# Copying out and laying down a forget gate's running sum before a memory step's second mix instead of after the step

## The chip, the cores and the metric

The kernel runs on one NeuronCore of a Trainium2 chip. The metric is the device time of one execution in microseconds, lower is better. TensorE does all matrix products and transposes and writes only to PSUM (eight banks of 128 partitions by 512 float32). ScalarE (ACT), VectorE (DVE), GpSimd (POOL) and SyncE (SP, which here only issues loads and stores) each run their own list of instructions in order, and meet through semaphores: an instruction that waits holds up all that stands behind it on its engine.

## The reference, cut to what matters

The model has two layers over 512 tokens of width 1024. The second one is what the change is in:

```
kvf = x @ kv_w                                   # keys, values and 12 forget-gate logits
f_logit = kvf[..., 2 * D_MIX:] + kv_b_f
logcum  = cumsum(log_sigmoid(f_logit), axis=1)   # running sum over the 512 tokens
z = x @ b_w_q                                    # queries: 12 heads, and 4 memory heads
mix = fox_attention(q, k_sh, v_sh, logcum)       # logit[t,s] = q_t.k_s/8 + logcum[t] - logcum[s]
mo  = memory_attention(qm, mk, mv)               # 4 heads, 256 memory tokens
y = concat([mix, mo]) @ w_o; LN; squared-ReLU MLP; LN
```

logcum[t] is constant along a row of the softmax and drops out, so only logcum[s] has to reach the scores: it does as an extra row of the key operand.

## The kernel before, in words

Float32 precision is made from float32r halves: each operand is split into hi (a copy that rounds, by ScalarE) and lo (whole minus hi, by VectorE, `rest` at L1462), and each product is three matmuls (hi·hi, hi·lo, lo·hi), all at L513.

Every engine has its own hand-written list. The second layer's mixer is a chain of **steps**, `pair_step`, one per pair of heads; a step handles eight units u (head u // 4, block u % 4 of 128 queries): scores into `sc[u % 2]`, maximum, exponential, normalization, transpose, split; then `attend(s, 0)` and `attend(s, 1)`, the probabilities times the values into the banks `pv`, which are copied out as `mix_hi` (ScalarE `attended`, L1137) and `mix_lo` (VectorE `attended`, L1545). Between the units TensorE runs **fillers**: parts of the next projections (weights `w_hi`, `w_lo`, into the banks `proj`).

The step before the six forget-gate pairs is `STEP_B`, the **double memory step**: it does all four memory heads at once (`double(s)` is true), a unit being one block of 128 queries for two heads. Its fillers make the query, key and value projections of the first forget-gate pair. At its end TensorE does, in this order: `attend` 0, `turn` 6, filler 8, `turn` 7, `cumulate()`, filler 9, `attend` 1 (the second mix), `turn_values`, and then the first filler and the scores of the next step.

`cumulate()` (L973) makes the running sum: eight matmuls of the split log gates with a triangular matrix into `sc[0]`, which signal `cum_done`. The way from there to the next step's scores:

1. ScalarE copies `sc[0]` to `cum` (L1434) and signals `f_act` 4.
2. VectorE waits for that and forms the lo part in rows 32 to 63 and 96 to 127 (`rest`, twice), signal `f_step` 6.
3. VectorE `cum_rows(pair)` (L1609 to L1616) waits for `f_step` 6 and writes the pair's rows into the key operand `kc` (two multiplications by `head_rows`), signal `row_ready`.
4. TensorE `scores` (L586) at unit 0 of the next step waits for `row_ready` (L598). At unit 1 it waits for `vt_ready` (L604): the value tile, turned by `turn_values` into `sc[1]` for this step, split into `v_hi` (L1194) and `v_lo` (L1657).

In the kernel before, 1 to 3 stand behind `pair_step(Pos(STEP_B), ...)` on ScalarE (L1433, L1434) and VectorE (L1951 to L1955), so behind the second mix's `mix_hi`, `mix_lo`, `v_hi` and `v_lo`. In the later steps `cum_rows(values)` is called inside `pair_step`, before `attended(s, 1)` (L1652). ScalarE's list goes on with the next step's weight split (`prepare`, L1066), VectorE's with the maximum (L1521) of unit 0. SyncE's loads wait for `w_split`, which VectorE's weight splits signal.

Of the kernel before, what the change touches and what calls it, by code (L numbers as in the profile page):

```python
# [63 lines left out]
def trunk_kernel(nc, x, mem, a_w_in, a_sgu_ln_g, a_sgu_ln_b, a_w_s, a_b_s, kv_w, kv_b_f, b_w_q,  # L64
# [41 lines left out]
    STEP_A, STEP_B, STEP_FOX, STEP_LAST = 0, 2, 3, 8  # L106
# [12 lines left out]
    with ctx:  # L119
        def psum(name):  # L120
            return ctx.enter_context(nc.psum_tensor(name, [P, 512], F32))

        def sem(name):
            return ctx.enter_context(nc.semaphore(name))
# [4 lines left out]
        def put(name, shape, dtype, offset=None):  # L129
            size = 4  # L130
            for n in shape[1:]:
                size *= n
            if offset is None:
                offset = base[0]
                base[0] += (size + 63) // 64 * 64
            assert offset + size <= nc.sbuf_usable_end, (name, offset + size)
            return nc.alloc_sbuf_tensor_at(name, shape, dtype, offset=offset)
# [82 lines left out]
        cum = put("cum", [P, T], F32R, B0 + 20 * K1)  # L220
# [53 lines left out]
        sc = [psum("sc0"), psum("sc1")]  # L274
# [33 lines left out]
        f_done, f_out, lf_zeroed, f_step, f_act, cum_done = sem("f_done"), sem("f_out"), sem("lf_zeroed"), sem("f_step"), sem("f_act"), sem("cum_done")  # L308
# [63 lines left out]
        def tr_index(s, u):  # L372
            return s.times(8, T_STEP[s.base >= STEP_B] + u)
# [4 lines left out]
        def fox(s):  # L378
            return STEP_FOX <= s.base <= STEP_LAST

        def double(s):

            return s.trip is None and s.base == STEP_B
# [13 lines left out]
        def keys(s, u):  # L397

            return u % TT + 1 if fox(s) else 2 * MT if double(s) else MT
# [659 lines left out]
        def _(act):  # L1059
            def prepare(b):  # L1060

                if b.trip is None and b.base >= B_DN[1][1] + 2 * KT:
                    return
                act.wait_ge(w_landed[b.slot], b.half(2) * 16)
                wait(act, w_used, space(b))
                act.copy(weights(b)[0], w_raw[:, b.slot]).then_inc(w_hi_ready, 1)  # L1066
# [11 lines left out]
            def turned_hi(t, target, source=None):  # L1078

                act.wait_ge(tr_done, t.at(1))  # L1080
                act.copy(target, tr[t.slot][:, :] if source is None else source).then_inc(tr_hi, 1)
# [50 lines left out]
            def turned_probs(s, u):  # L1132
                n, t = keys(s, u), tr_index(s, u)
                turned_hi(t, turned_places(s, u)[0],
                          tr[t.slot][:, 0:n * P].rearrange("p (j t) -> p j t", j=n))
# [26 lines left out]
            def pair_step(s, b=None, g=None, values=None, late=None):  # L1162

                mixing = b is not None and s.base < STEP_B
                reading = b is not None and s.base >= STEP_B
                for u in range(8):
                    if mixing and u in (0, 3, 6):
                        prepare(b.plus(u // 3 + 1))
                    if reading and u in (0, 4, 7):
                        prepare(b.plus((u + 2) // 3 + (u == 0)))  # L1170
                    if late is not None and u == 1:
                        prepare(late)
                    if ahead(s):
                        exponentials(s, u)
                    if u >= 2:
                        turned_probs(s, u - 2)
                    if not ahead(s):
                        exponentials(s, u)
                    if mixing and u in (2, 5):
                        step_projection(s, b.plus(u // 3), g.plus(u // 3), u // 3)  # L1180
                    if reading and u == 2:
                        for head in range(2):
                            fox_head(b, g, 0, head)
                    if reading and u in (5, 6):
                        fox_head(b.plus(1), g.plus(1), 1, u - 5)
                attended(s, 0)
                turned_probs(s, 6)
                turned_probs(s, 7)
                if b is not None:
                    step_projection(s, b.plus(2), g.plus(2), 2)  # L1190
                attended(s, 1)
                if values is not None:
                    act.wait_ge(vt_done, values.at(1))
                    act.copy(v_hi[:, values.slot], values_bank(s)[:, :].rearrange("p (t c) -> p t c", t=TT)).then_inc(vt_hi, 1)  # L1194
# [234 lines left out]
            for r in range(0, P, 32):  # L1429
                last = act.copy(lf_hi[:, :, r:r + HEADS], f_sp[:, :, :])  # L1430
            last.then_inc(f_act, 1)
            pair_step(Pos(STEP_B), Pos(B_FOX), Pos(G_FOX), values=Pos(0))
            act.wait_ge(cum_done, 1)  # L1433
            act.copy(cum[:, :], sc[0][:, :]).then_inc(f_act, 1)  # L1434
            with act.Fori(0, 2) as i:
                for j in range(2):
                    pair_step(Pos(STEP_FOX + j, i, 2), Pos(B_FOX + 3 * (j + 1), i, 6),
# [21 lines left out]
        def _(dve):  # L1459
            def rest(target, whole, hi):  # L1460

                return dve.tensor_tensor(target, whole, hi.bitcast(F32), ALU.subtract)  # L1462
# [146 lines left out]
            def cum_rows(pair):  # L1609

                dve.wait_ge(f_step, 6)
                for head in range(2):
                    rows = other_rows(head)
                    last = dve.tensor_scalar(kc[rows, pair.slot, head, :], cum[rows, :].bitcast(F32),
                                             head_rows[rows, bass.ds(pair.at(), 1)], None, ALU.mult)
                last.then_inc(row_ready, 1)  # L1616

            def pair_step(s, b=None, g=None, values=None, late=None):
                mixing = b is not None and s.base < STEP_B
                reading = b is not None and s.base >= STEP_B  # L1620
                if ahead(s):
                    row_max(s, 0)
                for u in range(8):
                    if not ahead(s):
                        row_max(s, u)
                    if mixing and u in (0, 3, 6):
                        prepare(b.plus(u // 3 + 1))
                    if reading and u in (0, 4):
                        prepare(b.plus(u // 4 + 1))
                    if late is not None and u == 1:  # L1630
                        prepare(late)
                    if ahead(s):
                        if u + 1 < 8:
                            row_max(s, u + 1)
                        normalize(s, u)
                    if u >= 2:
                        turned_probs(s, u - 2)
                    if not ahead(s):
                        normalize(s, u)
                    if s.base == STEP_A and 1 <= u <= TT:  # L1640
                        gate_norm(u - 1)
                    if reading and u in (2, 3):
                        fox_query(values, g, u - 2)
                    if reading and u == 6:
                        fox_key(values, g.plus(1), 0)
                turned_probs(s, 6)
                attended(s, 0)
                turned_probs(s, 7)
                if reading:
                    prepare(b.plus(3))  # L1650
                    fox_key(values, g.plus(1), 1)
                if fox(s) and values is not None:  # L1652
                    cum_rows(values)
                attended(s, 1)
                if values is not None:
                    dve.wait_ge(vt_hi, values.at(1))
                    rest(v_lo[:, values.slot], values_bank(s)[:, :].rearrange("p (t c) -> p t c", t=TT),  # L1657
                         v_hi[:, values.slot]).then_inc(vt_ready, 1)
# [235 lines left out]
            for j in range(PAIRS + 1):  # L1894
                if j == 2:
                    prepare(Pos(B_WO[0] + 1))
                for c in range(2):
# [6 lines left out]
                    for head in range(2):  # L1904
                        rows = slice(head * HALF, (head + 1) * HALF)
                        last = dve.tensor_tensor(gated(j, c)[rows].rearrange("p (n t) -> p n t", n=2), mixed[rows, :, head],
                                                 u_t[rows, j, c * 2 * P:(c + 1) * 2 * P].rearrange("p (n t) -> p n t", n=2), ALU.mult)
# [39 lines left out]
            for r in range(0, P, 32):  # L1947
                last = rest(lf_lo[:, :, r:r + HEADS], f_sp[:, :, :], lf_hi[:, :, r:r + HEADS])
            last.then_inc(f_step, 1)
            pair_step(Pos(STEP_B), Pos(B_FOX), Pos(G_FOX), values=Pos(0))  # L1950
            dve.wait_ge(f_act, 4)  # L1951
            for r in (32, 96):
                last = rest(cum[r:r + 32, :], sc[0][r:r + 32, :], cum[r:r + 32, :])
            last.then_inc(f_step, 1)
            cum_rows(Pos(0))  # L1955
            with dve.Fori(0, 2) as i:
                for j in range(2):
                    pair_step(Pos(STEP_FOX + j, i, 2), Pos(B_FOX + 3 * (j + 1), i, 6), Pos(G_FOX + 3 * (j + 1), i, 6),
                              values=Pos(j + 1, i, 2))
# [171 lines left out]
```

## Time and profile before

| | |
|---|---|
| device time, median of 3 runs | 1207.45 us (1206.73 to 1207.56) |
| the profiled execution | 1207.21 us |
| its span, first to last instruction | 1205.5 us |
| TensorE busy | 1161.2 us, 96% |
| VectorE busy | 632.7 us, 52% |
| ScalarE busy | 491.2 us, 41% |
| GpSimd busy | 129.3 us, 11% |
| mean granted TensorE clock | 0.992 of full speed |
| the chain that ended last | TensorE 74%, VectorE 4%, ScalarE 4%, issue 3% |

The span runs from the first to the last recorded instruction; the rest of the device time lies around it. Busy shares are means over stages with different limits. The double memory step lies at about 602 to 637 us of the span, the six forget-gate pairs follow until about 790 us, then the output projection and the second MLP. "PE" is TensorE's matmuls, "PEld" its weight loads.

### The profile page before, as it was taken

How to read it: one execution, taken by the hardware profiler on the slowest of the kernel's cores; microseconds unless marked ns; L12 is line 12 of the kernel's file. 1: busy time of each engine (PE TensorE's matmuls, PEld its weight loads, DVE VectorE, ACT ScalarE, POOL GpSimd, SP SyncE). 2: the span in 40 equal slices, each digit the busy share in tenths (PEclk: the TensorE clock that was granted, in tenths of full speed). 3: DMA queues.
4: the chain of work that ended last, by engine and by line, in shares of the span. 5: the costliest groups of instructions: out<-in, count | busy, mean ns of one | idle time of the engine just before them, and what ended most of it. 6: DMA issues, size and time to landing. Idle time of an engine off the chain costs nothing.

```text
span 1205.5 us, 16763 instructions
## 1 busy us (share of the span) xinstructions
PE 1161.2 (96%) x5888; PEld 976.6 (81%) x5888; DVE 632.7 (52%) x1032; ACT 491.2 (41%) x852; POOL 129.3 (11%) x156
## 2 busy tenths in 40 slices
PE   5998999999999999999998999999999999999997
PEld 5777779888888888789877888878888888888886
DVE  4477766644332445345576777866544323445226
ACT  4445535634211333224665555635543212334120
POOL 2300025100000000023300000026200000000000
PEclk9999999999999999999998999999999999999999
DMA  7422122333323333332311122212333333333332
GB/s 219 134 70 71 53 90 86 88 89 103 105 87 104 88 101 91 105 88 73 86 35 53 54 70 62 60 53 84 93 104 90 102 104 87 88 98 93 105 105 87
DMA packets 185590, 107.22 MB, mean 89 GB/s; under 512 B 4482, under 2 KB 180162, under 8 KB 185540
## 3 DMA queue, kind: packets, MB, share of 16 engines
q1 hardware_dynamic: 180112, 99.36, 28.5%
q10 hardware_dynamic: 5428, 7.18, 1.9%
q8 instruction: 32, 0.52, 0.2%
q14 instruction: 18, 0.15, 0.0%
HBM read 104.43 MB, written 2.10 MB: 88 GB/s over the span
## 4 chain that ended last, share of the span: by engine, by line
PE 74%; DVE 4%; ACT 4%; issue 3%; POOL 1%; DMA 0%; DVEq 0%; ACTq 0%; POOLq 0%; SPq 0%
PE proj L513 59%; PE pv L513 3%; PE sc L513 2%; PE proj L846 2%; PE pv L846 2%; PE tr L846 2%; PE sc L846 2%; PE tr L561 1%; DVE w_lo L1462 1%; ACT w_hi L1066 1%; ACT x L1232 1%; ACT x_hi L1234 1%; POOL total L2054 0%; DVE split_lo L1462 0%; POOL total L2064 0%
## 5 line engine op out<-in xcount | busy, mean ns | idle before, releaser
L1462 DVE TENSOR_TENSOR w_lo<-w_raw,w_hi 128x1024 fp32r<-128x1024 f32 x173 | 219.6, 1270 | 172.3 <-ACT w_hi L1066 124.2
L513 PE MATMUL proj<-x_hi,w_hi 128*128 128x512 f32 (+1 forms) x768 | 300.5, 393 | 1.9 <-ACT relu L1097 1.0
L513 PE MATMUL proj<-x_hi,w_lo 128*128 128x512 f32 (+1 forms) x768 | 295.9, 386 | 0.0
L513 PE MATMUL proj<-x_lo,w_hi 128*128 128x512 f32 (+1 forms) x768 | 289.8, 384 | 0.0
L1066 ACT CAST w_hi<-w_raw 128x1024 fp32r<-128x1024 f32 x160 | 166.9, 1044 | 168.6 <-PE proj L513 166.9
L513 PEld LDWEIGHTS proj<-x_hi,w_hi 128*128 128x128 f32 x768 | 146.1, 190 | 28.9 <-ACT x_hi L1234 2.2
L513 PEld LDWEIGHTS proj<-x_hi,w_lo 128*128 128x128 f32 x768 | 145.8, 190 | 29.2
L513 PEld LDWEIGHTS proj<-x_lo,w_hi 128*128 128x128 f32 x768 | 143.1, 189 | 25.7
L513 PE MATMUL proj<-h_hi,w_hi 128*128 128x512 f32 (+1 forms) x384 | 146.4, 381 | 2.5 <-DVE w_lo L1462 2.5
L513 PE MATMUL proj<-h_lo,w_hi 128*128 128x512 f32 (+1 forms) x384 | 146.0, 380 | 0.0
L513 PE MATMUL proj<-h_hi,w_lo 128*128 128x512 f32 (+1 forms) x384 | 146.0, 380 | 0.0
L1755 DVE TENSOR_TENSOR h_raw<-relu 128x512 f32<-128x512 f32 x64 | 44.3, 692 | 157.7 <-ACT relu L1097 157.7
L1097 ACT ACTIVATE relu<-proj 128x512 f32<-128x512 f32 x64 | 38.2, 597 | 196.0 <-PE proj L513 196.0
L513 PEld LDWEIGHTS proj<-h_hi,w_hi 128*128 128x128 f32 x384 | 72.2, 188 | 16.8 <-DVE w_lo L1462 3.1
L513 PEld LDWEIGHTS proj<-h_lo,w_hi 128*128 128x128 f32 x384 | 72.2, 188 | 13.8
L513 PEld LDWEIGHTS proj<-h_hi,w_lo 128*128 128x128 f32 x384 | 72.2, 188 | 13.7
L1129 ACT ACTIVATE probs<-sc,neg_max 128x128 f32<-128x128 f32 (+2 forms) x64 | 33.0, 516 | 55.9 <-DVE neg_max L1521 54.9
L2005 POOL TENSOR_TENSOR x_lo<-x,x_hi 128x256 fp32r<-128x256 f32 (+1 forms) x56 | 48.5, 875 | 58.0 <-ACT x L1230 24.8
L1462 DVE TENSOR_TENSOR h_lo<-h_raw,h_hi 128x512 f32 (+1 forms) x64 | 44.3, 692 | 14.9 <-ACT h_hi L1246 14.4
L2054 POOL TENSOR_TENSOR total<-x 128x512 f32<-128x512 f32 x3 | 4.5, 1499 | 440.9 <-DVE x L1672 440.9
L513 PE MATMUL proj<-mix_hi,w_hi 128*128 128x256 f32 (+1 forms) x128 | 45.8, 358 | 2.5 <-DVE w_lo L1462 2.2
L1665 DVE SCALAR_TENSOR_TENSOR x<-x,proj 128x512 f32 (+1 forms) x22 | 15.1, 687 | 61.0 <-PE proj L513 61.0
(344 smaller groups left out, 1805.4 us busy)
## 6 DMA issues: line engine op xcount, KB each, us to landing
w_raw<-in_w_up SPq DMA_DIRECT2D x64, 512.0 KB, 4.0
w_raw<-in_w_down SPq DMA_DIRECT2D x64, 512.0 KB, 3.6
w_raw<-in_w_o SPq DMA_DIRECT2D x16, 512.0 KB, 3.6
w_raw<-in_a_w_in SPq DMA_DIRECT2D x14, 512.0 KB, 3.8
w_raw<-in_kv_w SPq DMA_DIRECT2D x12, 512.0 KB, 3.9
w_raw<-in_mem_w_kv SPq DMA_DIRECT2D x8, 512.0 KB, 4.9
w_raw<-in_b_w_q SPq DMA_DIRECT2D x8, 512.0 KB, 3.6
x_nat<-in_x ACTq DMA_DIRECT2D x2, 1024.0 KB, 11.4
```

Source lines behind the costliest of these rows:

```text
L513: last = pe.matmul(target, lhs, rhs, start=start and n == 0, stop=stop and n == len(terms) - 1)
L561: last = pe.transpose(tr[t.slot][0:n, at:at + rows], piece, ident[0:rows, 0:rows])
L846: last = pe.matmul(rows_of[t][n][:, :], lhs, rhs, start=False, stop=stop and m == 2, skip_group_check=True)
L1066: act.copy(weights(b)[0], w_raw[:, b.slot]).then_inc(w_hi_ready, 1)
L1097: act.activation(target, proj[g.slot][:, 0:target.shape[-1]], function).then_inc(proj_free[g.slot], 1)
L1129: act.activation(probs[:, u % 2, 0:n], sc[u % 2][:, 0:n], ACT.Exp, bias=neg_max[:, u:u + 1], accum_out=row_sum[:, u:u + 1]).then_inc(exp_d ...
L1232: act.activation(x32[:, k, own], x32[:, k, own], ACT.Identity, **gain).then_inc(fin_ready, 1)
L1234: act.copy(x_hi[:, k, own], x32[:, k, own]).then_inc(x_hi_ready, 1)
L1462: return dve.tensor_tensor(target, whole, hi.bitcast(F32), ALU.subtract)
L1665: dve.scalar_tensor_tensor(out=tile if target is None else target, in0=tile, scalar=ALPHA if first else 1.0, in1=proj[g.slot][:, :], op0=A ...
L1755: dve.tensor_tensor(raw, wide, wide, ALU.mult).then_inc(relu_sq, 1)
L2005: pool.tensor_tensor(x_lo[:, k, own], x32[:, k, own], x_hi[:, k, own].bitcast(F32), ALU.subtract).then_inc(x_ready, 1)
```

## The change

ScalarE's copy moves from behind the step to a place in it ahead of the value projection's copy (`step_projection`) and of the second mix's. VectorE's two subtractions and `cum_rows` move to ahead of the second mix's `mix_lo`, behind the key's second half (`fox_key`). The condition of the `cum_rows` call widens so that it holds for the double step too. No instruction, wait or buffer is added or dropped, and TensorE's, GpSimd's and SyncE's lists are as before.

```diff
 # ScalarE, pair_step
                 attended(s, 0)
                 turned_probs(s, 6)
                 turned_probs(s, 7)
+                if double(s):
+                    act.wait_ge(cum_done, 1)
+                    act.copy(cum[:, :], sc[0][:, :]).then_inc(f_act, 1)
                 if b is not None:
                     step_projection(s, b.plus(2), g.plus(2), 2)
                 attended(s, 1)
 # ScalarE, the list
             pair_step(Pos(STEP_B), Pos(B_FOX), Pos(G_FOX), values=Pos(0))
-            act.wait_ge(cum_done, 1)
-            act.copy(cum[:, :], sc[0][:, :]).then_inc(f_act, 1)
 # VectorE, pair_step
                 if reading:
                     prepare(b.plus(3))
                     fox_key(values, g.plus(1), 1)
-                if fox(s) and values is not None:
+                if double(s):
+                    dve.wait_ge(f_act, 4)
+                    for r in (32, 96):
+                        last = rest(cum[r:r + 32, :], sc[0][r:r + 32, :], cum[r:r + 32, :])
+                    last.then_inc(f_step, 1)
+                if s.base >= STEP_B and values is not None:
                     cum_rows(values)
                 attended(s, 1)
 # VectorE, the list
             pair_step(Pos(STEP_B), Pos(B_FOX), Pos(G_FOX), values=Pos(0))
-            dve.wait_ge(f_act, 4)
-            for r in (32, 96):
-                last = rest(cum[r:r + 32, :], sc[0][r:r + 32, :], cum[r:r + 32, :])
-            last.then_inc(f_step, 1)
-            cum_rows(Pos(0))
```

## Rows read from the trace of the kernel before

**Rows 1.** Waits of TensorE, whole span: who waited, for whom, total us, times, longest.
```profile
PE sc L513 <- DVE kc L1614: 3.5, 1, 3.5
```
**Rows 2.** TensorE's timeline, end of the double step: start us, duration us, instruction, [idle before <-releaser].
```profile
629.24 0.22 PE L513 MATMUL sc<-tri_r,lf_hi 128*128 128x128 f32 x1
629.30 0.27 PE L513 MATMUL sc<-tri_r,lf_lo 128*128 128x128 f32 x1
...
636.32 0.39 PE L513 MATMUL proj<-x_lo,w_hi 128*128 128x512 f32 x1
636.54 0.40 PE L513 MATMUL proj<-x_hi,w_lo 128*128 128x512 f32 x1
640.45 0.44 PE L513 MATMUL sc<-kc,qc 128*128 128x128 f32 x1 [3.51 <-DVE kc L1614]
```
**Rows 3.** VectorE's timeline there, same columns.
```profile
632.35 0.70 DVE L1462 TENSOR_TENSOR kc<-proj,ks 64x512 fp32r<-64x512 f32 x1
635.66 1.39 DVE L1462 TENSOR_TENSOR mix_lo<-pv,mix_hi 64x512 fp32r<-64x512 f32 x2 [2.61 <-ACT mix_hi L1142]
637.08 0.69 DVE L1462 TENSOR_TENSOR v_lo<-sc,v_hi 128x512 fp32r<-128x512 f32 x1
637.80 1.40 DVE L1462 TENSOR_TENSOR cum<-sc,cum 32x512 fp32r<-32x512 f32 x2
639.23 0.98 DVE L1614 TENSOR_SCALAR kc<-cum,head_rows 64x512 fp32r<-64x512 f32 x2
```
**Rows 4.** ScalarE's timeline there.
```profile
627.86 1.11 ACT L1081 CAST pn_hi<-tr 128x512 fp32r<-128x512 f32 x2
631.73 0.60 ACT L1097 ACTIVATE v_tmp<-proj 128x512 f32<-128x512 f32 x1 [2.76 <-PE proj L513]
634.45 1.17 ACT L1142 CAST mix_hi<-pv 64x512 fp32r<-64x512 f32 x2 [2.13 <-PE pv L513]
...
636.13 0.59 ACT L1434 CAST cum<-sc 128x512 fp32r<-128x512 f32 x1
636.61 1.06 ACT L1066 CAST w_hi<-w_raw 128x1024 fp32r<-128x1024 f32 x1
```
**Rows 5.** GpSimd's timeline, its last instruction before the next step.
```profile
624.31 0.61 POOL L2102 CAST ks<-ks 64x512 fp32r<-64x512 f32 x1 [1.93 <-ACT ks L1159]
```
**Rows 6.** TensorE's timeline, one step later (the second forget-gate pair), and the third's start.
```profile
669.38 0.39 PE L513 MATMUL proj<-x_hi,w_lo 128*128 128x512 f32 x1
669.60 0.22 PE L513 MATMUL sc<-kc,qc 128*128 128x128 f32 x1
...
671.99 0.28 PE L513 MATMUL sc<-kc,qc 128*128 128x256 f32 x1
...
673.73 0.27 PE L561 MATMUL tr<-ident,probs 128*128 128x128 f32 x1
...
696.10 0.22 PE L513 MATMUL sc<-kc,qc 128*128 128x128 f32 x1
```
**Rows 7.** VectorE's timeline in that step, from unit 0's maximum.
```profile
670.08 0.29 DVE L1521 TENSOR_REDUCE neg_max<-sc 128x1 f32<-128x128 f32 x1 [0.54 <-PE sc L513]
670.29 1.22 DVE L1462 TENSOR_TENSOR w_lo<-w_raw,w_hi 128x1024 fp32r<-128x1024 f32 x1
...
671.62 0.29 DVE L1537 TENSOR_SCALAR probs<-probs,inv_sum 128x128 f32<-128x128 f32 x1
```
**Rows 8.** Windows: us, then busy (instructions) of PE, PEld, DVE, ACT, POOL, clock granted, DMA share, GB/s.
```profile
636.00:639.20 3.20, 0.94 (x5) 0.42 (x3) 3.11 (x5) 1.67 (x3) 0.00 (x0) 1.00 0.00 0
639.20:646.00 6.80, 5.55 (x16) 4.71 (x17) 2.80 (x7) 0.46 (x2) 0.00 (x0) 0.50 0.27 77
547.00:550.50 3.50, 1.83 (x16) 1.63 (x15) 3.25 (x3) 1.17 (x2) 1.05 (x1) 1.00 0.01 4
799.60:803.00 3.40, 3.40 (x10) 2.62 (x9) 0.34 (x1) 0.00 (x0) 0.00 (x0) 0.51 0.87 245
844.00:847.40 3.40, 3.40 (x18) 3.40 (x17) 1.46 (x5) 1.28 (x2) 0.34 (x1) 0.50 0.90 266
```
**Rows 9.** TensorE's timeline: three other pauses.
```profile
549.18 0.39 PE L513 MATMUL proj<-h_hi,w_hi 128*128 128x256 f32 x1 [1.67 <-DVE w_lo L1462]
798.26 0.50 PE L513 MATMUL proj<-mix_hi,w_hi 128*128 128x512 f32 x1 [1.76 <-DVE w_lo L1462]
843.58 0.38 PE L513 MATMUL proj<-x_hi,w_hi 128*128 128x256 f32 x1 [0.44 <-ACT x_hi L1234]
```

## The prediction

> **What bounds the kernel now.** I read the table of engine shares first. TensorE is busy 1161.2 of 1205.5 us, so the kernel is a stream of matmuls with 44.3 us of holes, and a change that leaves TensorE's list alone can gain only by closing holes, or by what a hole does to the clock. The list of TensorE's waits came second: one of the holes is a single wait of 3.5 us for `kc`, written by the line of `cum_rows` [rows 1]. Third, the timelines of the engines around it. TensorE issues the last filler matmul at 636.54 and the next step's first score matmul at 640.45, idle 3.51 us between [rows 2]. In that time VectorE works without a break: `mix_lo`, `v_lo`, `cum`, `kc`, from 635.66 to 640.2 [rows 3]. But what it does from 637.80 on, the running sum, has had its input in PSUM since 629.30 + 0.27 = 629.57 [rows 2]: it is late because of its place in the list and not because of data. Fourth, the windows by clock: at 636.00 to 639.20 TensorE is busy 0.94 of 3.20 us at full clock (2.4 GHz), and then, from 639.20 to 646.00, the granted clock is 0.50 (1.2 GHz) [rows 8]. So the hole costs twice: its own length, and a slow stretch behind it.
>
> **The moved work on ScalarE.** One copy, 0.59 us alone, 0.48 from its start to the next one's [rows 4]. Before, it stands at 636.13, behind `v_hi`. In its new place ScalarE is free at 627.86 + 1.11 = 628.97, the data is there at 629.57, so it runs from about 629.6 to 630.2. Behind the new wait on ScalarE stand the value projection's copy `v_tmp`, then `mix_hi` and `v_hi`. `v_tmp` waits for TensorE until 631.73 after 2.76 us of idleness [rows 4], so the copy lies wholly in that idleness with 1.5 us left. That cover cannot go away by itself, since TensorE runs `cumulate()` before the filler that `v_tmp` waits for. If it did, each 0.1 us would delay `v_tmp` by 0.1, for which TensorE waits in `turn_values`. Cost taken: 0, with 0 and 0.5 us (the whole copy exposed) as ends. At the old place the copy's absence lets `w_hi` start 0.48 earlier, at 636.13, which nobody awaits that early: a gain of 0.
>
> **The moved work on VectorE.** Two subtractions and two multiplications, from 637.80 to 639.23 + 0.98 = 640.21, 2.41 us in all [rows 3]. In the new place they follow the key's second half, which ends at 632.35 + 0.70 = 633.05. The wait for the copy (630.2) is long met. So they run from 633.05 to about 635.47. Behind them stands `mix_lo`, which waits for ScalarE's `mix_hi` until 635.66 after 2.61 us of idleness [rows 3]. The 2.41 us fit into the 2.61 with some 0.2 us left. That is a narrow fit, so what if it fails: `mix_lo` and `v_lo` end later by the excess. `v_lo` ends at 637.08 + 0.69 = 637.77. It is wanted by the scores of unit 1, which in the undisturbed step come 671.99 - 669.60 = 2.39 us behind those of unit 0 [rows 6], so at 636.77 + 2.39 = 639.16 in the new kernel. There are 1.4 us of slack behind the 0.2. Cost taken: 0. Ends: 0, and 1.0 us if the moved work took 2.6 us longer than its rows. No queue of DMA is passed: the change issues none. SyncE's loads wait for weight splits, and the last one of the step stands ahead of the moved work on VectorE.
>
> **What goes.** With `row_ready` at 635.5, TensorE doesn't wait at unit 0. The other things awaited there are earlier: GpSimd's last copy of key rows ended at 624.92 [rows 5], and the key bank came free with the subtraction that ended at 633.05 [rows 3]. The score matmul then follows the filler at the filler's own pace: 636.54 - 636.32 = 0.22 in the step itself, 669.60 - 669.38 = 0.22 one step later [rows 2, 6]. I take 636.54 + 0.23 = 636.77. First term: 640.45 - 636.77 = **3.68 us**.
>
> Second term, the slow stretch. From the first score matmul of this step to that of the next one it takes 669.60 - 640.45 = 29.15 us; the following step, same instructions and granted the full clock, takes 696.10 - 669.60 = 26.50 [rows 2, 6]. If the hole goes and the clock stays up, the first step takes 26.50 too: **2.65 us**. This agrees with the windows: 5.55 us of busy time at half clock is 2.8 us of excess [rows 8].
>
> What is late next? VectorE, relative to TensorE. In the undisturbed step it starts unit 0's maximum 0.48 us after the first score matmul, splits a weight tile, and finishes the normalized probabilities at 671.62 + 0.29, so 2.31 us after it. TensorE wants them for its transpose at 673.73, 4.13 us after it [rows 6, 7]. Here `v_lo` holds VectorE until 637.77, 1.0 us after the score matmul, so all of this slides by 0.5 us, or 0.7 with a step of the loop's own instructions, against a slack of 1.8. The weight tile itself has its `w_hi` at 636.13 + 1.06 = 637.2, before VectorE comes to it. I therefore expect no new hole of more than 0.2 us. Of all later waits none is on an absolute time: loads wait for splits, splits for weights used, so the whole rest moves up with TensorE.
>
> **The sum.** 3.68 + 2.65 = 6.33 us. The profiled execution took 1207.21 us (a span of 1205.5 and 1.7 around it), which gives 1200.88; the median of the runs lies 0.24 higher, so the forecast is 1207.45 - 6.33 = **1201.1 us**.
>
> **The clock, page against row.** The trace shows full clock during the 3.51 us pause and half clock behind it until 646.00. It also shows half clock behind a pause of 1.76 us (799.60 to 803.00) and behind one of 0.44 (844.00 to 847.40), but full clock around one of 1.67 at 549 [rows 8, 9]. So the length of a pause alone does not say whether the clock falls. The Trainium skill, "TensorE: Matmul & The Clock Gate", section "What's actually happening", says that the gate's looks are free-running, not tied to the kernel's own start. By that rule a program that reaches its later pauses 6.3 us earlier may lose the clock at other ones than now. The trace, with its three unlike cases, agrees as far as it goes.
>
> **Rivals.**
>
> *A, only the hole goes.* The double step has short pauses of its own and many transposes, and the clock could fall somewhere near even without the hole, as it did behind the 0.44 us pause [rows 9]. Against it: from 628 to 636.8 TensorE has no pause at all in its timeline, and with the hole closed it goes on at the same density. Then only 3.68 is gained: 1203.8 us.
>
> *B, the later slow stretches change.* Each of the two at 799.60 and 844.00 lasts 3.4 us at half clock [rows 8], so one more or one less is worth 1.7 us. One less: 1207.45 - 6.33 - 1.7 = 1199.4; one more: 1202.8. The stretch at 844 follows a pause of 0.44 us and looks marginal, the pause of 1.67 at 549 lies before the change and stays as it is. I hold one less for somewhat more likely than one more.
>
> *C, no effect.* The wait moves to another operand of the same scores, or `cum_rows` is held by something that I don't see. Against it: every other input is there by 633.05. The time stays within 0.2% of 1207.45, the most that a measurement of this kernel can't tell from no change (2.4 us).
>
> *D, slower.* The place is VectorE's list ahead of the second mix. If the moved work, reading PSUM while ScalarE and TensorE use their banks, ran so long that `v_lo` came late for unit 1's scores, the hole would reappear there. To eat the gain it must reopen a hole of 3.68 us with its slow stretch: `v_lo` not before 639.16 + 3.68 = 642.8, 5.1 us later than now, so the moved work would need 2.41 + 0.2 + 5.1 = 7.7 us instead of 2.41. At 9 us the time would be 1208.7. For it speaks only that the fit is narrow; against it that ScalarE's and TensorE's lists show nothing that touches `sc[0]` at 633 to 635.5.
>
> **How the numbers follow.** Forecast, both terms and later clock as now: 0.62. B: 0.20 (0.12 for one less, 0.08 for one more). A: 0.11. C: 0.05. D: 0.02. All of the forecast, B and A is more than 0.2% faster, which gives 0.93 faster, 0.05 the same, 0.02 slower. The range holds the forecast, B on both sides and A: from 1199.2 (B with one stretch less, less 0.2 for the spread of the runs) to 1203.9 (A).
>
> **What would show it.** In the new profile `cum` on ScalarE starts at about 629.6 and on VectorE at about 633.1, and `kc` of L1614's successor ends by 635.5 with `mix_lo` still at 635.7: if `mix_lo` has moved, the VectorE fit was wrong. TensorE's wait for `kc` is gone from the list, the first score matmul stands at 636.8, and the windows from 636 to 646 have clock 1.00. If the step from there to the next takes 29 us, the second term was wrong and A holds. If a wait for `v_lo` or for the probabilities appears at 638 to 641, the sum is too large by its length. A difference of 1.7 us that appears only behind 790 us is B.

## The result, and the profile after

The changed kernel takes 1200.39 us (median of 6 runs, 1199.33 to 1200.48) against 1207.22 us for the kernel before on the same chip (6 runs, 1206.17 to 1208.16). The ratio is 0.9946, 95% interval [0.9933, 0.9958]: 6.5 us less, between 5.1 and 8.1. The forecast was 1201.1 and faster. Measured again on another chip, the changed kernel took 1200.95 us (median of 5 runs, 1199.09 to 1204.40) against 1205.69 (13 runs), ratio 0.9963 [0.9948, 0.9977]: 4.5 us less, between 2.8 and 6.3; a sixth run took 4067.55 us, for a reason that nothing here shows, and is left out as a slow one. The two intervals overlap from 5.1 to 6.3 us. The traces of the kernel before, further down, show how much of its time changes from one execution to the next.

TensorE's timeline of the changed kernel, where [rows 2] had the pause (called the hole from here on):

```profile
637.06 0.39 PE L513 MATMUL proj<-x_lo,w_hi 128*128 128x512 f32 x1
637.29 0.40 PE L513 MATMUL proj<-x_hi,w_lo 128*128 128x512 f32 x1
637.52 0.22 PE L513 MATMUL sc<-kc,qc 128*128 128x128 f32 x1
...
639.91 0.28 PE L513 MATMUL sc<-kc,qc 128*128 128x256 f32 x1
```

The first score matmul comes 0.23 us behind the filler's last one. This execution reached the double step 0.77 us later than the other (where it lost that is shown in the last section), so it stands at 637.52 and not at 636.77. The next pair's follows at 663.98.

VectorE's timeline there, against [rows 3]:

```profile
633.10 0.70 DVE L1463 TENSOR_TENSOR kc<-proj,ks 64x512 fp32r<-64x512 f32 x1
633.83 1.39 DVE L1463 TENSOR_TENSOR cum<-sc,cum 32x512 fp32r<-32x512 f32 x2
635.25 0.98 DVE L1615 TENSOR_SCALAR kc<-cum,head_rows 64x512 fp32r<-64x512 f32 x2
636.40 1.39 DVE L1463 TENSOR_TENSOR mix_lo<-pv,mix_hi 64x512 fp32r<-64x512 f32 x2 [0.17 <-ACT mix_hi L1142]
637.83 0.69 DVE L1463 TENSOR_TENSOR v_lo<-sc,v_hi 128x512 fp32r<-128x512 f32 x1
638.44 0.28 DVE L1522 TENSOR_REDUCE neg_max<-sc 128x1 f32<-128x128 f32 x1
```

The four moved operations fill what was 2.61 us of idleness ahead of `mix_lo`, and 0.17 us of it are left. `mix_lo` has not moved: 636.40 less 0.77 is 635.63, against 635.66.

ScalarE's timeline, against [rows 4]:

```profile
630.35 0.59 ACT L1191 CAST cum<-sc 128x512 fp32r<-128x512 f32 x1 [0.64 <-PE sc L513]
632.47 0.60 ACT L1097 ACTIVATE v_tmp<-proj 128x512 f32<-128x512 f32 x1 [1.54 <-PE proj L513]
635.20 1.18 ACT L1142 CAST mix_hi<-pv 64x512 fp32r<-64x512 f32 x2 [2.13 <-PE pv L513]
636.40 0.59 ACT L1197 CAST v_hi<-sc 128x512 fp32r<-128x512 f32 x1
636.88 1.06 ACT L1066 CAST w_hi<-w_raw 128x1024 fp32r<-128x1024 f32 x1
```

The copy waits 0.64 us for the sum's last matmul, and ScalarE is idle another 1.54 us before `v_tmp` wants it. Two windows of the changed kernel, with the columns of [rows 8]:

```profile
636.00:639.20 3.20, 3.20 (x17) 2.68 (x16) 2.98 (x6) 2.36 (x5) 0.00 (x0) 1.00 0.15 43
639.20:646.00 6.80, 6.80 (x35) 5.66 (x34) 4.67 (x13) 2.96 (x9) 1.22 (x2) 1.00 0.28 80
```

TensorE is busy all through and the granted clock is 1.00 (2.4 GHz), where it was 0.50 (1.2 GHz) from 639.20 on.

**The ledger of the two profiled executions.** I cut both spans at three events of TensorE: the double step's first scores, the first scores of the first forget-gate pair, and those of the second pair.

| | before | changed | difference |
|---|---|---|---|
| start to the double step's first scores | 601.86 | 602.63 | +0.77 |
| double step (D) | 38.59 | 34.89 | -3.70 |
| first forget-gate step (S) | 29.15 | 26.46 | -2.69 |
| from there to the end | 535.90 | 534.72 | -1.18 |
| span | 1205.5 | 1198.7 | -6.8 |

D and S together hold 6.39 us, against 6.33 forecast. The other two lines belong to no changed instruction; together they are another 0.41 us in favour of the changed kernel, which the forecast did not contain. D + S is therefore what I compare in the experiments, beside the times of whole runs.

### The profile page after: what moved, and what is told of

Same layout as the page of the kernel before. It is cut to its first block, busy times and chain, and to the rows that moved or that the text cites. A ratio compares the mean times of both kernels' runs of the same rounds, so it can differ in the third digit from the quotient of the medians.

```text
span 1198.7 us, 16763 instructions
## 1 busy us (share of the span) xinstructions
PE 1157.2 (97%) x5888; PEld 974.3 (81%) x5888; DVE 632.4 (53%) x1032; ACT 491.7 (41%) x852; POOL 129.6 (11%) x156
## 4 chain that ended last, share of the span: by engine, by line
PE 74%; DVE 4%; ACT 4%; issue 3%; POOL 1%; DMA 0%; DVEq 0%; ACTq 0%; POOLq 0%; SPq 0%
PE proj L513 59%; PE pv L513 3%; PE sc L513 2%; PE proj L846 2%; PE sc L846 2%; PE pv L846 2%; PE tr L846 2%; PE tr L561 1%; DVE w_lo L1463 1%; ACT w_hi L1066 1%; ACT x L1235 1%; ACT x_hi L1237 1%; POOL total L2055 0%; DVE split_lo L1463 0%; ACT probs L1125 0%
```

## The experiments

The first four were timed side by side on one chip, 12 runs each against 35 of the kernel before (median 1206.63 us); the changed kernel again, the longer block and the step's start on another, with 5 to 7 runs each against 13 (1205.69 us). Each has one trace unless more are named.

**ScalarE's move alone.** The kernel before, with one edit:

```diff
 # ScalarE, pair_step, behind turned_probs(s, 7)
+                if double(s):
+                    act.wait_ge(cum_done, 1)
+                    act.copy(cum[:, :], sc[0][:, :]).then_inc(f_act, 1)
 # ScalarE, the list, behind pair_step(Pos(STEP_B), ...)
-            act.wait_ge(cum_done, 1)
-            act.copy(cum[:, :], sc[0][:, :]).then_inc(f_act, 1)
```

> The kernel before with ScalarE's copy of the running sum moved early and VectorE's part left behind the step. Theory (the hole is made by VectorE's list, where the sum stands behind mix_lo and v_lo): kc still ends at 640.2, TensorE still waits 3.5 us for it, the half-clock stretch behind it stays, and the time is that of the kernel before within 0.3 us. Rival (ScalarE's late copy is part of what makes the rows late): the hole shrinks by up to 0.5 us and the time by as much.

Ratio 0.9997 [0.9986, 1.0007]. Its timeline of TensorE:

```profile
640.82 0.45 PE L513 MATMUL sc<-kc,qc 128*128 128x128 f32 x1 [3.51 <-DVE kc L1615]
```

D 38.55, S 29.25. The hole is the same to the hundredth, and half clock follows it: the theory holds, an early copy alone is worth nothing.

**VectorE's move alone.** The changed kernel, with ScalarE's copy back in its old place (the two edits above, reversed).

> The changed kernel with ScalarE's copy put back behind v_hi, VectorE's part left ahead of mix_lo. Theory: VectorE now stands waiting for the copy, which comes at 636.1 to 636.7 on the time axis of the kernel before, so kc ends near 639.2 and the first scores start near 639.4 instead of 640.45: a hole of 2.6 us. If a hole of that size still brings the half clock, the time is 1.0 us under before (1206.2); if it does not, 3.7 us under (1203.5). No second hole at the scores of unit 1 at half clock, since v_lo ends at 641.3. Rival (one engine's move is enough): the full gain, 1200.4.

The first trace, VectorE and then TensorE:

```profile
636.87 1.40 DVE L1462 TENSOR_TENSOR cum<-sc,cum 32x512 fp32r<-32x512 f32 x2 [3.71 <-ACT cum L1434]
638.30 0.98 DVE L1614 TENSOR_SCALAR kc<-cum,head_rows 64x512 fp32r<-64x512 f32 x2
...
640.74 0.69 DVE L1462 TENSOR_TENSOR v_lo<-sc,v_hi 128x512 fp32r<-128x512 f32 x1
```
```profile
639.52 0.30 PE L513 MATMUL sc<-kc,qc 128*128 128x128 f32 x1 [2.47 <-DVE kc L1614]
```

VectorE stands 3.71 us at the wait for the copy, and the hole is 2.47 us, as the theory had it (2.6). D 37.56, S 26.52, clock full. By this trace the kernel should be 3.7 us faster than the one before, but the ratio over 12 runs is 0.9998 [0.9985, 1.0010], so between 1.8 us less and 1.2 us more. The medians (1204.66 against 1206.63) lie 2.0 us apart, just outside that interval, so what this kernel gains in time stays uncertain between nothing and 2 us. Either way it is less than the trace says, which led to the last experiments.

**The hole filled.** The kernel before, with matmuls that take TensorE through its wait:

```diff
 # TensorE, the list
             pair_step(Pos(STEP_B), Pos(B_FOX), Pos(G_FOX), values=Pos(0))
+            for n in range(14):
+                pe.matmul(proj[(G_FOX + 2) % 2][:, :], ident_r[:, :], x_hi[:, n % KT], start=True, stop=True)
```

> The kernel before with 14 more matmuls of 128x512, whose result nothing reads, between turn_values and the next step's first filler, so that TensorE works through the time in which it waited. The first scores cannot start earlier than before. Theory (the hole costs its length and, apart from that, 2.65 us of half clock behind it): the 14 take 3.2 us of the 3.5, the clock stays at 1.00 behind them, and the time is 2.65 us under before, 1204.6. Rival (the half-clock stretch belongs to the double step as a whole and not to the hole): windows behind 639 still show 0.50, and the time is that of before, 1207.2.

TensorE's timeline and the window behind it:

```profile
635.22 3.47 PE L1044 MATMUL proj<-x_hi,ident_r 128*128 128x512 f32 x14
...
641.07 0.30 PE L513 MATMUL sc<-kc,qc 128*128 128x128 f32 x1 [0.34 <-DVE kc L1616]
```
```profile
639.20:646.00 6.80, 6.46 (x33) 5.20 (x32) 4.30 (x10) 1.29 (x5) 0.00 (x0) 1.00 0.24 70
```

The scores come no earlier (D 38.55), yet S is 26.59 instead of 29.15: in this trace work that nobody needs gives back 2.6 us. It is one trace, but the others say the same: half clock follows in all six traces with a pause of 3.51 us here (the five of the kernel before and the one of ScalarE's move alone) and stays away in all five in which TensorE has work up to the scores, or nearly so (this one, two of the changed kernel, the longer block, the step's start). So the slow stretch comes from the pause, and the two terms of the forecast are separate things. The ratio is 0.9984 [0.9970, 0.9998], 1.9 us less, between 0.2 and 3.6, where 2.65 was expected.

**The rows behind the step.** The changed kernel with `cum_rows(Pos(0))` put back into VectorE's list behind `pair_step(Pos(STEP_B), ...)`, and the condition of the call inside the step back to `fox(s)`.

> The changed kernel with the two subtractions left early but cum_rows put back behind v_lo. Theory: kc ends 0.98 us behind v_lo, near 638.8 on the time axis of the kernel before, the first scores start near 639.0, a hole of 2.2 us instead of 3.5. Its length alone gives 1.4 us over before; with the half clock avoided 4.1. So 1205.8 if a hole of 2.2 us here still costs the clock, 1203.1 if not. Rival (the subtractions are the costly part and the rows come free): 1200.4.

```profile
637.76 0.98 DVE L1615 TENSOR_SCALAR kc<-cum,head_rows 64x512 fp32r<-64x512 f32 x2
```
```profile
638.98 0.30 PE L513 MATMUL sc<-kc,qc 128*128 128x128 f32 x1 [2.08 <-DVE kc L1615]
```

The hole is 2.08 us, D 37.15 and S 26.54. In length it is as expected; this trace shows the full clock behind it. The ratio, 0.9988 [0.9976, 0.9999], is 1.4 us less (0.1 to 2.9), nearer to the expectation with the half clock than to the other, 4.1, which lies outside the interval: the same disagreement as above (the medians, 1203.73 against 1206.63, give 2.9). The rival (subtractions costly, rows free) falls: the two multiplications behind `v_lo` alone keep 2.1 us of the hole.

**A longer VectorE block.** The changed kernel with:

```diff
 # VectorE, pair_step, behind cum_rows(values)
+                if double(s):
+                    for tile in (f_turned, tri_f):
+                        for r in (0, 64):
+                            rest(tile[r:r + 64, :], cum[r:r + 64, :].bitcast(F32), cum[r:r + 64, :])
```

> The changed kernel with four more VectorE subtractions of 64x512 between cum_rows and mix_lo, 2.76 us by the 0.69 of such rows, whose result nothing reads; row_ready is signalled ahead of them. It tries the narrow fit. Theory: the first 0.17 us go into VectorE's idleness ahead of mix_lo, mix_lo and v_lo end 2.6 us later, the scores of unit 1 wait for v_lo with 1.4 us of slack, so TensorE gets a hole of 1.2 us there and none at unit 0; time 1.2 us over the changed kernel. Rival (the second mix's mix_lo is on the path by itself): a hole of the full 2.6 us. If VectorE's later start on unit 0 counts instead, the hole is at the first transpose of the next step.

VectorE, then TensorE:

```profile
638.02 1.39 DVE L1463 TENSOR_TENSOR mix_lo<-pv,mix_hi 64x512 fp32r<-64x512 f32 x2
639.45 0.69 DVE L1463 TENSOR_TENSOR v_lo<-sc,v_hi 128x512 fp32r<-128x512 f32 x1
```
```profile
636.60 0.22 PE L513 MATMUL sc<-kc,qc 128*128 128x128 f32 x1
...
640.28 0.36 PE L513 MATMUL sc<-kc,qc 128*128 128x256 f32 x1 [1.13 <-DVE v_lo L1463]
```

No pause at unit 0, one of 1.13 us at unit 1, for `v_lo`, where 1.2 was expected. The rival, a hole of the full 2.6 us, falls. D is 34.93 (34.89 in the changed kernel), S 28.01, so 1.56 more, and the clock is full. The narrow fit is thus no cliff: of 2.8 us of added work 1.6 are paid. The hole fits a slack of 0.17 and then 1.4 us, with one length tried; S grew by 0.4 us more than the hole, and where those went was not followed up. The ratio is 0.9971 [0.9960, 0.9982], against 0.9963 [0.9948, 0.9977] for the changed kernel measured beside it (medians 1202.00 and 1200.95): the times alone could not tell the two apart.

**The changed kernel again.**

> The changed kernel again, on the same chip as the next two and with more runs. The first call's runs of the kernel before spread over 1202.3 to 1209.9 us. Theory: hole and slow stretch are both gone, so 1200.4 to 1201.1 against a median before of 1206.6 to 1207.2, a difference of 5.5 to 6.8 us. Rival (part of the 6.8 us measured first was the luck of the clock elsewhere in the kernel): near 3.7 to 5 us, while the trace still shows the first scores directly behind the filler and clock 1.00 there.

1200.95 against 1205.69, ratio 0.9963: 4.5 us, where the first measurement gave 6.5. The trace shows D 34.89 and S 26.45, within 0.01 of the first. So the local effect in the changed kernel repeats, while the estimate of the whole difference moved by 2 us. That is in the rival's range, though the interval (2.8 to 6.3) reaches into the theory's too, and it was a reason to trace the kernel before again rather than the changed one.

**Four more traces of the kernel before,** with nothing edited.

> The kernel before again, for its trace alone (first of four looks). Measured over many runs the change gave less than its local 6.4 us on the second chip. Theory (the hole costs its 3.68 us and 2.65 us of half clock in every execution, and the rest of the spread is luck elsewhere): from the first scores of the first forget-gate pair to those of the second it takes 29.1 to 29.3 us in all four. Rival (the half clock behind the hole is itself a matter of luck): that stretch takes from 26.5 to 29.2 us, different from look to look, while the hole itself stays 3.5 us long.

> Second look at the kernel before, for its trace alone; the same two expectations as for the first.

> Third look at the kernel before, for its trace alone; the same two expectations as for the first.

> Fourth look at the kernel before, for its trace alone; the same two expectations as for the first.

| kernel before | hole | D | S | D + S | span |
|---|---|---|---|---|---|
| the one shown in the rows | 3.51 | 38.59 | 29.15 | 67.74 | 1205.5 |
| trace 1 | 3.51 | 38.57 | 28.12 | 66.69 | 1205.5 |
| trace 2 | 3.51 | 38.59 | 29.12 | 67.71 | 1204.7 |
| trace 3 | 3.51 | 38.54 | 28.15 | 66.69 | 1205.5 |
| trace 4 | 3.51 | 38.59 | 28.13 | 66.72 | 1202.7 |
| changed kernel, two traces | none | 34.89, 34.89 | 26.46, 26.45 | 61.35, 61.34 | 1198.7, 1198.7 |

The hole is always 3.51 us. The half clock is there in all five, but in two sizes: S is 2.7 us over 26.45 in two, 1.7 us in three. In the two it lasts 6.8 us and begins inside the pause (in the rows at 639.20, 1.25 us before the scores); in the three it lasts 3.4 us. In trace 1, one of the three, the clock falls only when the pause is over, so the first scores still run at the full clock:

```profile
641.06 0.30 PE L513 MATMUL sc<-kc,qc 128*128 128x128 f32 x1 [3.51 <-DVE kc L1614]
641.19 0.27 PE L513 MATMUL sc<-causal_r,ident_r 128*128 128x128 f32 x1
```
```profile
640.00:642.00 2.00, 0.94 (x5) 0.88 (x6) 1.18 (x4) 0.05 (x1) 0.00 (x0) 0.87 0.02 4
642.00:644.00 2.00, 2.00 (x6) 1.54 (x5) 1.40 (x3) 0.41 (x2) 0.00 (x0) 0.50 0.00 0
```

With the mean D + S of the five, 67.11 us, the changed kernel's local gain is 5.8 us, and the filled hole's (D + S 65.14) is 2.0, against 1.9 measured.

**A second trace of VectorE's move alone.**

> The kernel with only VectorE's part moved, once more for its trace. Its first trace showed a hole of 2.47 us and the full clock behind it, while its runs spread from 1203.1 to 1208.8 us. Theory (whether the clock falls behind a pause depends on where the pause meets the chip's looks): the hole is 2.5 us again, and the stretch to the next pair's scores takes 26.5 us or, with half clock, up to 28.5. Rival (a pause of this length never costs the clock here): 26.5 again.

```profile
639.49 0.45 PE L513 MATMUL sc<-kc,qc 128*128 128x128 f32 x1 [2.46 <-DVE kc L1614]
```
```profile
639.20:646.00 6.80, 6.51 (x18) 5.41 (x19) 4.23 (x9) 1.01 (x4) 0.00 (x0) 0.50 0.28 78
```

The same program and the same pause (2.46 against 2.47), but here half clock for 6.8 us and S 29.58 instead of 26.52. So the clock took 3.1 us in this execution and nothing in the first. It even went past the expected 28.5. D + S is 64.08 in the one and 67.15 in the other, so against the 67.74 of the kernel before this kernel wins 3.7 us in one execution and 0.6 in another; against the 66.7 of three of its five traces it would win 2.6 or lose 0.4. The means (65.62 of two, 67.11 of five) are 1.5 us apart, which the interval allows. That is how its first trace and its ratio can both be right. How often each occurs I can't say from two traces.

**The same reordering at the step's start.** The changed kernel with ScalarE's split of the first weight tile behind unit 0's exponential, and VectorE's behind unit 1's maximum:

```diff
 # ScalarE, pair_step
-                    if reading and u in (0, 4, 7):
+                    if reading and u in ((4, 7) if double(s) else (0, 4, 7)):
 # ... behind exponentials(s, u)
+                    if double(s) and u == 0:
+                        prepare(b.plus(1))
 # VectorE, pair_step
-                    if reading and u in (0, 4):
+                    if reading and u in ((1, 4) if double(s) else (0, 4)):
```

> The changed kernel with the same kind of reordering at the start of the double step: ScalarE's split of the first weight tile behind the exponential of unit 0 instead of ahead of it, VectorE's part of it behind unit 1's maximum. TensorE waits 2.0 us for unit 0's probabilities there. Theory: the copy's 1.04 us leave the chain to the exponential, which starts 0.9 to 1.0 us earlier, and the pause shrinks to about 1.0; the time falls by up to 1.0 us if VectorE keeps up in the units behind it. Rival (VectorE is the bound of this step as a whole): the pause shrinks and the following units' pauses grow by as much, no change at the step's end.

The first two of TensorE's pauses in it, then two of those of the changed kernel, then one of the longer block, whose step starts as the changed kernel's does:

```profile
606.15 0.66 PE L561 MATMUL tr<-ident,probs 128*128 128x128 f32 x4 [1.06 <-DVE probs L1535]
607.88 0.50 PE L513 MATMUL proj<-x_hi,w_hi 128*128 128x512 f32 x1 [0.60 <-DVE w_lo L1465]
```
```profile
607.84 0.66 PE L561 MATMUL tr<-ident,probs 128*128 128x128 f32 x4 [2.02 <-DVE probs L1533]
618.87 0.50 PE L513 MATMUL proj<-x_hi,w_hi 128*128 128x512 f32 x1 [1.57 <-DVE w_lo L1463]
```
```profile
606.85 0.66 PE L561 MATMUL tr<-ident,probs 128*128 128x128 f32 x4 [1.99 <-DVE probs L1533]
```

The first pause shrinks by the 0.96 us of the theory, a new one of 0.60 for the weight tile appears, and D ends at 34.85 against 34.89. The clocks of these two traces differ in this step (a slow stretch at 608 to 612 in this one, none in the other), but the longer block's trace has the same slow stretch, the pause of 1.99 us, and D 34.93. Beside it the edit shortens the pauses by 0.33 us and D by 0.08. So next to nothing was won by the step's end, as the rival had it. The ratio 0.9951 [0.9938, 0.9963] overlaps that of the changed kernel. I don't count it as a better version.

## Why the prediction was right

Point by point:

- **The list and not the data made the rows late.** Shown. The copy alone gives nothing in the trace, VectorE's part alone leaves 2.5 us of the hole, both leave none. The hole followed the end of `kc` in each of four arrangements (3.51, 2.47, 2.08, none).
- **ScalarE's copy costs nothing.** Shown: `mix_hi` moved by 0.75 us, as much as TensorE's own stream did, with 1.54 us of idleness left ahead of `v_tmp`.
- **VectorE's 2.41 us fit into 2.61 with 0.2 left.** Measured 0.17. The slack behind it, 1.4 us at unit 1, was tried with one longer block: 1.2 us of pause expected, 1.13 measured.
- **First term, 3.68 us.** D fell by 3.70, and in no trace of the kernel before or the changed one did it vary by over 0.05.
- **Second term, 2.65 us.** The mechanism is shown, by the filled hole above all. The size was that of one execution: 2.7 us in two of five traces of the kernel before, 1.7 in three. The mean of the five is 2.1. With it the local gain is 5.8 us, and the forecast's 6.33 was at the high end of 5.3 to 6.4. A single trace doesn't show that spread; four more did. The prediction also read the rows as full clock during the pause and half clock behind it, but [rows 8] have 0.50 from 639.20 on and the scores start at 640.45, so the clock fell inside the pause; the term is not touched by that, since it was taken from S.
- **The size of the whole.** That 6.5 us came out so near 6.33 is in part luck: the profiled pair held 0.41 us from stretches that no edit touches, and its kernel before was one of the two with the longer slow stretch. The second measurement's 4.5 us [2.8, 6.3] just misses 6.33 and holds the 5.8. Its time of 1200.95 agrees with the forecast of 1201.1 while the kernel before was 1.8 us faster there than the 1207.45 that the forecast started from.
- **What is late next.** As forecast nothing: no wait of TensorE in the changed kernel between 626 and 668. VectorE began unit 0's maximum 0.92 us after the first scores, and the transpose still came 4.13 us after them, as in the undisturbed step.
- **Rival B, the later slow stretches.** It happened in the profiled execution in addition to the forecast. The stretch of 799.60 to 803.00 [rows 8] has no counterpart: behind the same pause of 1.76 us the clock stays. I held that for a 12% case. It is missing in both traces of the changed kernel, but also in traces 2 and 4 of the kernel before, where the later one, between 840 and 848, lasts twice as long instead. From the second pair's first scores to the end it takes 534.7 us in those two and in both of the changed kernel, and 535.9 to 536.3 in the other three of the kernel before. So such stretches come and go without any change to the kernel; whether the earlier arrival makes this one rarer, as I had put it, is open. From the changed kernel:

```profile
792.69 0.50 PE L513 MATMUL proj<-mix_hi,w_hi 128*128 128x512 f32 x1 [1.76 <-DVE w_lo L1463]
```
```profile
793.00:797.00 4.00, 4.00 (x19) 3.29 (x18) 1.72 (x3) 0.00 (x0) 0.00 (x0) 1.00 0.66 176
```

- **Rivals A, C and D** did not occur. A's slow stretch is in neither trace of the changed kernel. The moved work took 2.40 us (633.83 to 636.23), where D needed 7.7. D's way of failing was tried in the longer block: the hole reappears exactly at the scores of unit 1, and 2.8 us of extra work cost 1.6.

The rule that the gate's looks are not tied to the kernel's start (the Trainium skill, "TensorE: Matmul & The Clock Gate", "What's actually happening") fits what the traces show: pause 2.47 and 2.46 us in one program, full clock behind one and half behind the other. That the gate's looks are the reason is not shown; no trace here records them.

## What to carry to other kernels

A result that waits in PSUM behind other work of an in-order list can cost twice: the time that the engine which needs it last stands idle, and a slow stretch of its clock; look for a place where both the copying engine and the splitting engine stand idle anyway, and move every link of the chain, for one link alone can be worth nothing. Price a TensorE pause as its length plus a slow stretch, and take the second from several executions, since here it was 1.7 or 2.7 us behind one and the same pause of 3.51 us, and 0 or 3.1 behind one of 2.5. To judge an edit whose effect is smaller than the spread of whole runs, cut several traces at fixed events around it and compare those stretches: D repeated to 0.05 us where whole runs of one kernel differed by 7. S repeated only where the clock did: to 0.01 us in the changed kernel, to 1.0 in the kernel before.

## What the runs showed of the hardware

The time of one and the same kernel moves by several microseconds: 35 runs of the kernel before on one chip lay between 1202.29 and 1209.93 us with mean clocks of 0.990 to 0.995. The mean clock explains only part of that: runs at 0.995 took from 1202.29 to 1206.51 us, runs at 0.992 from 1204.74 to 1209.93. What makes up the rest no run here shows. The slow stretches change place from execution to execution. The two profiled ones shown here, first the changed kernel and then the one before, at the same stretches of the first layer, which no edit touches:

```profile
24.00:27.00 3.00, 3.00 (x16) 3.00 (x15) 1.37 (x3) 2.16 (x3) 2.15 (x2) 0.50 0.62 175
194.50:198.00 3.50, 3.50 (x19) 3.50 (x19) 1.30 (x5) 0.26 (x2) 0.00 (x0) 0.54 0.00 0
```
```profile
24.00:27.00 3.00, 3.00 (x28) 2.95 (x26) 1.36 (x3) 2.33 (x4) 1.66 (x2) 1.00 0.64 180
194.50:198.00 3.50, 3.50 (x32) 3.50 (x32) 2.08 (x8) 0.98 (x3) 0.35 (x1) 1.00 0.00 0
```

What they cost can be read between pauses that both traces have. Around the first, TensorE's pauses before and after are these, again the changed kernel first:

```profile
22.68 0.39 PE L513 MATMUL proj<-memt_hi,w_hi 128*128 128x256 f32 x1 [2.94 <-DVE w_lo L1463]
28.51 0.39 PE L513 MATMUL proj<-memt_hi,w_hi 128*128 128x256 f32 x1 [0.32 <-DVE w_lo L1463]
```
```profile
23.18 0.39 PE L513 MATMUL proj<-memt_hi,w_hi 128*128 128x256 f32 x1 [2.94 <-DVE w_lo L1462]
29.00 0.39 PE L513 MATMUL proj<-memt_hi,w_hi 128*128 128x256 f32 x1 [1.81 <-DVE w_lo L1462]
```

It takes 5.83 us from the one to the other with the slow stretch and 5.82 without: the slow clock only took the place of a wait for a weight split. Around the second, from the pause at 190.69 to the one at 218.01 it is 27.32 us, and 26.17 (191.25 to 217.42) in the kernel before, so that one cost 1.15 us. The changed kernel's execution was 0.50 us ahead at the first pause; the +0.77 us of the ledger's first line are -0.50, +0.01, +1.15 and 0.11 us in between and behind.

The double memory step shows the same. In the kernel before it has a slow stretch at 608 to 612 in the profile of the rows and none in trace 1, and D is 38.59 and 38.57. Without it TensorE runs ahead and then waits 1.57 us for a weight split (at 618.73 in trace 1, at 618.87 in the changed kernel's trace above): VectorE sets the pace there, and TensorE's slower clock only takes the place of a wait.
